# Six mix products in front of the retention, and two tiles' router input made by GpSimd

## The reference, cut to what matters

```python
mod = (silu(c) @ w_ada + b_ada)          # six vectors of 1024: sh1, sc1, g1, sh2, sc2, g2
proj = (x * (1 + sc1) + sh1) @ w_in
y_ssd, y_rg, y_ret = ssd(proj), rglru(proj), retention(proj)     # 1024, 512, 512 features
mix = concat([y_ssd, y_rg, y_ret]) @ w_out                       # 2048 x 1024
x = layernorm(ALPHA * x + (1 + g1) * mix)
h2 = x * (1 + sc2) + sh2
x = layernorm(ALPHA * x + (1 + g2) * moe(h2))                    # router, then 32 experts, top 2 of one group
```

## Time and profile before

| | |
|---|---|
| median of three runs | 1937.51 us |
| the profiled execution: its time, its span | 1933.65 us, 1931.8 us |
| TensorE busy | 1540.0 us (80%) |
| VectorE busy | 752.8 us (39%) |
| ScalarE busy | 348.1 us (18%) |
| GpSimd busy | 113.7 us (6%) |
| chain that ended last | PE 47%, DMA 39%, DVE 6% |

### The profile page before, as it was taken

How to read it: one execution, slowest core, us unless ns; L and a number is a source line. 1 busy time by engine, 2 the same in 40 slices (tenths; PEclk the granted TensorE clock), 3 DMA queues, 4 the chain that set the end, 5 groups by cost and what they waited for, 6 DMA issues and landing times.

```text
span 1931.8 us, 29459 instructions
## 1 busy us (share of the span) xinstructions
PE 1540.0 (80%) x11754; PEld 830.8 (43%) x11754; DVE 752.8 (39%) x1685; ACT 348.1 (18%) x773; POOL 113.7 (6%) x162
## 2 busy tenths in 40 slices
PE   5999999888767677668699999998887767667782
PEld 2764544434433334334266554353453334333441
DVE  0343657567212222122525356666732222122235
ACT  1235311121101111100123532110311111011010
POOL 3000012101000000000020000211000000000000
PEclk8999998988988888888899899998888888788896
DMA  9445346517899999999935433654669999999991
GB/s 328 143 175 179 121 122 205 219 71 290 364 427 427 428 429 428 429 428 427 384 111 198 155 121 121 207 170 163 283 268 427 428 429 429 428 428 428 428 427 78
DMA packets 93463, 567.53 MB, mean 294 GB/s; under 512 B 7061, under 2 KB 7917, under 8 KB 68034
## 3 DMA queue, kind: packets, MB, share of 16 engines
q1 hardware_dynamic: 81666, 532.05, 67.6%
q0 software_dynamic: 11712, 34.32, 6.3%
HBM read 550.53 MB, written 15.81 MB: 293 GB/s over the span
## 4 chain that ended last, share of the span: by engine, by line
PE 47%; DMA 39%; DVE 6%; ACT 2%; issue 2%; SPq 2%; DVEq 2%; PEldq 0%; PEld 0%; ACTq 0%
DMA ring<-in_exp_w_up 37%; PE ps L1445 10%; PE ps L962 9%; PE ps L937 9%; PE ps L1183 3%; PE ps L944 2%; PE ps L1308 2%; DMA ring<-in_w_out 2%; PE ps L863 1%; PE ps L805 1%; PE ps L1420 1%; PE ps L1153 1%; DMA ring<-in_w_ada 1%; PE ps L1088 1%; PE ps L1129 1%
## 5 line engine op out<-in xcount | busy, mean ns | idle before, releaser
L1445 PE MATMUL ps<-ring,xTb 128*32 128x256 f32 x4224 | 326.9, 478 | 240.8 <-DMA ring<-in_exp_w_up 235.6
L1445 PEld LDWEIGHTS ps<-ring,xTb 128*32 128x32 f32 x4224 | 163.0, 136 | 404.1 <-issue 359.8
L2522 DVE TENSOR_TENSOR hb<-sg,ps 128x128 f32<-128x128 f32 x66 | 25.0, 379 | 492.6 <-ACT sg L1784 492.6
L962 PE MATMUL ps<-ring,hT 128*128 128x512 f32 x384 | 171.4, 598 | 0.0
L937 PE MATMUL ps<-hT,ring 128*128 128x288 f32 x640 | 165.4, 418 | 5.9 <-ACT hT L1565 2.4
L1420 PE MATMUL ps<-sel,h_tm 128*128 128x128 f32 (+1 forms) x912 | 163.5, 306 | 0.0
L1420 PEld LDWEIGHTS ps<-sel,h_tm 128*128 128x128 f32 x912 | 125.2, 189 | 53.9 <-issue 26.2
L937 PEld LDWEIGHTS ps<-hT,ring 128*128 128x128 f32 x640 | 122.7, 195 | 44.1 <-issue 9.7
L1459 PE MATMUL ps<-ring,hTb 128*32 128x256 f32 x2112 | 131.0, 389 | 5.1 <-DVEq L2525 5.1
L1784 ACT ACTIVATE sg<-ps 128x128 f32<-128x128 f32 x66 | 18.3, 278 | 596.2 <-PE ps L1445 596.2
L2530 DVE COPY ys<-ps 32x256 f32<-32x256 f32 x132 | 56.0, 424 | 166.0 <-PE ps L1459 164.8
(11 more groups left out here) (444 smaller groups left out, 1617.8 us busy)
## 6 DMA issues: line engine op xcount, KB each, us to landing
ring<-in_exp_w_gate SPq DMA_DIRECT2D x66, 2048.0 KB, 18.8
ring<-in_exp_w_up SPq DMA_DIRECT2D x66, 2048.0 KB, 23.3
ring<-in_exp_w_down SPq DMA_DIRECT2D x66, 2048.0 KB, 24.8
ring<-in_w_ada SPq DMA_DIRECT2D x24, 2048.0 KB, 11.4
ring<-in_w_in SPq DMA_DIRECT2D x22, 2048.0 KB, 9.1
ring<-in_w_out SPq DMA_DIRECT2D x8, 2048.0 KB, 14.7
h0s<-in_state_ssd POOLq DMA_DIRECT2D x16, 512.0 KB, 7.1
out_ssd_s<-h0s POOLq DMA_DIRECT2D x16, 512.0 KB, 5.5
```

The lines of the kernel that those rows point to most:

```text
L962: last = mm(o[:, :], hT[:, k, T0[i]:T0[i] + P], w[:, k, :], start=(k == 0), stop=(k == KT - 1))
L1445: last = mm(ps[32 * j:32 * j + 32, b, 0:2 * P], xTb[:, k, m * BLK:(m + 1) * BLK], w[:, 0:2, k * D_EXPERT + j * P:k * D_EXPERT + (j + 1) * ...
```

## The change: what it does

Two things, in both layers.

1. TensorE does all six products mix_a(0..2, 0..1) before it turns q and k, and releases slots 1 and 2 right behind them. The places in the retention that they leave are filled by ada blocks: block 8 behind the scores of tile 0, block 9 before the turning of tile 0's result, block 10 behind ri of tile 1, and only block 11 in the part of the sample states. The bank list and ScalarE's list follow the same order.
2. h2 of tiles 0 and 2 is made by GpSimd: it waits for sh2 and sc2, then for each of the two tiles a product, a drain and a sum. VectorE signals the tiles that it has normalised and goes on with the last half of tile 1. TensorE waits for GpSimd's signal before it turns tiles 0 and 2, and VectorE waits for it before it writes `rt`, which lies over sc2.

```diff
--- before.py
+++ after.py
@@ ret_steps @@
     if i == 0:
-        out += [(("mix_a", 1, 1), "A"), (("rs", i), "D"), (("mix_a", 2, 0), "A"), (("ri", i), "D"), (("mix_a", 2, 1), "A")]
+        out += [(("ada", 8), "A"), (("rs", i), "D"), (("ri", i), "D")]
     elif i == 1:
-        out += [(("ro", i), "D"), (("rs", i), "D"), (("ada", 8), "A"), (("yrt", 0), "A"), (("ri", i), "D"), (("ada", 9), "A")]
+        out += [(("ro", i), "D"), (("rs", i), "D"), (("ada", 9), "A"), (("yrt", 0), "A"), (("ri", i), "D"), (("ada", 10), "A")]
     else:
-        out += [(("rt", b), "D") for b in range(4)] + [(("yrt", 1), "A"), (("ada", 10), "A"), (("ada", 11), "A")]
+        out += [(("rt", b), "D") for b in range(4)] + [(("yrt", 1), "A"), (("ada", 11), "A")]
@@ bank_plan @@
-    out += [(("yt", 2, a), "A") for a in range(2)] + [(("mix_a", 1, 0), "A")]
+    out += [(("yt", 2, a), "A") for a in range(2)]
+    out += [(("mix_a", i, a), "A") for i in (1, 2) for a in range(2)]
@@ signals @@
-        h2_ready = sig("h2_ready", NT + 1)
+        h2_ready = sig("h2_ready", 2)
+        h2_few = sig("h2_two_tiles_ready", 2)
+        x_normed = sig("two_tiles_normed", 2)
@@ GpSimd, behind the loads of ln1_g and ln1_b @@
+                pool.wait_ge(*takes(l, ("ms", 6)))
+                idle["pool"].stand(pool)
+                for n_, i in enumerate(NORM_ORDER[:2]):
+                    R_, w_ = ROWS[i], int(i == 2)
+                    pool.wait_ge(x_normed.sem, x_normed.at(l, n_ + 1))
+                    pool.tensor_tensor(h_tm[0:R_, i, :].rearrange("r (k p) -> r k p", k=KT),
+                                       x_tm[0:R_, i, :].rearrange("r (p k) -> r k p", k=KT),
+                                       sc2[0:R_, w_, :].rearrange("r (k p) -> r k p", k=KT), ALU.mult)
+                    pool.drain()
+                    pool.tensor_tensor(h_tm[0:R_, i, :], h_tm[0:R_, i, :], sh2[0:R_, w_, :], ALU.add
+                                       ).then_inc(h2_few.sem, 1)
                 pool.wait_ge(x1_done.sem, x1_done.at(l, 1))
@@ TensorE @@
                 turn_rows(h_tm, "yt", 2)
-                mix_a(1, 0)
+                for i in (1, 2):
+                    for a in range(2):
+                        mix_a(i, a)
+                free_slot(n_out)
+                free_slot(n_out + 1)
...
                     if i == 0:
-                        mix_a(1, 1)
+                        pe.wait_ge(bias_in.sem, bias_in.at(l, 32))
+                        ada_here(8)
...
                             if q:
-                                ada_here(10)
                                 ada_here(11)
...
-                    if i == 0:
-                        mix_a(2, 0)
                     if i == 1:
-                        pe.wait_ge(bias_in.sem, bias_in.at(l, 32))
-                        ada_here(8)
+                        ada_here(9)
                         turn_ret(0)
...
-                    if i == 0:
-                        mix_a(2, 1)
-                        free_slot(n_out)
-                        free_slot(n_out + 1)
                     if i == 1:
-                        ada_here(9)
+                        ada_here(10)
...
                 for n_, i in enumerate(NORM_ORDER[:2]):
-                    pe.wait_ge(h2_ready.sem, h2_ready.at(l, n_ + 1))
+                    pe.wait_ge(h2_few.sem, h2_few.at(l, n_ + 1))
                     turn_rows(h_tm, "h2t", i)
@@ VectorE @@
                         norm((i,), 2 * NT + 1 + NORM_ORDER.index(i), ln1_in)
-                        if i == 2:
-                            dve.wait_ge(*takes(l, ("ms", 6)))
-                            modulate(0)
-                            modulate(2)
+                        dve.sem_inc(x_normed.sem, 1)
                 D().then_inc(x1_done.sem, 1)
+                dve.wait_ge(*takes(l, ("ms", 6)))
...
                 pref = over(C("pref"), NT, 1)
+                dve.wait_ge(h2_few.sem, h2_few.at(l, 2))
                 V.memset(rt[:, 0], 0.5)
```

More of the change, by code:

```diff
@@ L1372, in _ @@
                 for a in range(2):
-                    pe.wait_ge(h2_ready.sem, h2_ready.at(l, NT + a))
+                    pe.wait_ge(h2_ready.sem, h2_ready.at(l, a + 1))
                     turn_half(1, a)
@@ L1708, in _ @@
                 take_rows(hT, "yt", 2)
-                take_mix_a(1, 0)
+                for i in (1, 2):
+                    for a in range(2):
+                        take_mix_a(i, a)
                 for i in range(NT):
@@ L1717, in take_ret @@
                     cp(yreT[:, :, T0[i]:T0[i] + R_], o[:, 0:4 * R_].rearrange("p (k t) -> p k t", k=4)).then_inc(TA, 1)
-                take_mix_a(1, 1)
-                take_mix_a(2, 0)
+                take_ada((8,))
                 rstd(NT + 1, ROWS[0], 0, RET_HEADS)
-                take_mix_a(2, 1)
                 act.wait_ge(ada_folded.sem, ada_folded.at(l, 1))
                 cp(adaf, ps[:, 7, :]).then_inc(adaf_ready.sem, 1)
-                take_ada((8,))
+                take_ada((9,))
                 take_ret(0)
                 rstd(NT + 2, ROWS[1], 0, RET_HEADS)
-                take_ada((9,))
+                take_ada((10,))
                 take_ret(1)
-                take_ada((10, 11))
+                take_ada((11,))
                 rstd(NT + 3, ROWS[2], 0, RET_HEADS)
@@ L2275, in _ @@
                 mods(range(4, 6))
-                def modulate(i):
-                    R_, w_ = ROWS[i], int(i == 2)
-                    tt(h_tm[0:R_, i, :].rearrange("r (k p) -> r k p", k=KT),
-                       x_tm[0:R_, i, :].rearrange("r (p k) -> r k p", k=KT),
-                       sc2[0:R_, w_, :].rearrange("r (k p) -> r k p", k=KT), ALU.mult)
-                    D()
-                    tt(h_tm[0:R_, i, :], h_tm[0:R_, i, :], sh2[0:R_, w_, :], ALU.add).then_inc(h2_ready.sem, 1)
                 if l == 0:
```

## The result

The changed kernel takes 1952.61 us (median of 4 runs, 1949.62 to 1954.86) against 1937.10 (1934.17 to 1939.25): a ratio of 1.0090 with a 95% interval of 1.0073 to 1.0106. The medians differ by 15.5 us, and the ratio stands for 14 to 21. The forecast was 1940.1, within 1930.5 to 1947.5. It is outside that range.

What follows compares the result with a forecast made beforehand. The prediction took the path from the retention to the first expert as the bound, experts alternating between TensorE and weight landings. Part 1 at 0 and part 2 at 2 x 1.3 gave 1937.51 + 2.6 = 1940.1 us, range 1930.5 to 1947.5.

Steps and rivals of the forecast that it cites:

- Part 1, 0 us: Retention to mix(0): reordering the six products turns the wait for weights into an equal wait for a bank; 0 us.
- VectorE's serial list: Retention and sample states: VectorE's work runs later, fourth state by 6.1 us, fifth by 5.2 in layer 0, 4.9 in layer 1.
- The wait for the seventh state's bank: Start of mix(0): its first half waits for this bank, taken at 392.7, so TensorE starts at 392.8.
- The price of the two products, kept at 16.42: At mix(0): the two products keep their slow start and still take 16.42 us.
- Rivals C and D: At mix(0): C, full clock, -2.4 per layer, 1935.3, chance 0.15; D, VectorE's list not late, 1926.0, chance 0.06.
- rival B: At h2: GpSimd is as fast as VectorE; -2.3 per layer, 1932.9, chance 0.14.
- Part 2, "the middle, 11.0": At h2 of tiles 0 and 2: GpSimd's four instructions take 11.0 us, fillers before the logits start +1.3 per layer.
- rival A: At h2: GpSimd and VectorE take turns at the same memory, tile 2 2.5 later; +3.8 per layer, 1945.1, chance 0.27.
- The high end (14.7, +5.0 per layer): At h2: GpSimd handles one operand after another with longer hand-overs, 14.7 us; +5.0 per layer, 1947.5.
- Whatever comes before the first expert moves the end one for one: Expert part of each layer: a delay ahead of the first expert shifts the end by the same amount.
- The sum: Whole kernel: 0 plus 2 x 1.3 = +2.6 us on the median 1937.51, giving 1940.1.

Runs made afterwards that it cites:

- part1_only: Kernel before with only the six mix products moved in front, h2 left with VectorE; ratio 1.0007.
- p1_fill2: Kernel before with the six products in front and filler products in TensorE's waits for h2 and around the rank matmuls, second measurement; ratio 0.9976.
- part2_only: Kernel before with only h2 of tiles 0 and 2 given to GpSimd, mix products where they were; ratio 1.0043.
- gp_tile2: Kernel before with six products in front, GpSimd making only tile 2's h2, an early small GpSimd product, and fillers around the rank matmuls; ratio 0.9966.
- after_again: The changed kernel measured once more, for a second profile; ratio 1.0093.
- warm: Changed kernel plus an 8-column product and drain on GpSimd ahead of its wait for the first tile, behind that for sc2; ratio 1.0084.
- fill_gp: Changed kernel with filler products in TensorE's long waits for GpSimd; ratio 1.0070.
- gp_alone: Changed kernel with VectorE waiting for GpSimd's second tile before tile 1's last half; ratio 1.0109.
- fill_rank: Changed kernel with eight fillers for seven ahead of the rank matmuls and three more behind them, before the diagonal's rows; ratio 1.0021.
- p1_trim: Kernel before with six products in front and fillers in TensorE's waits, but one filler for three ahead of the logits, one for two behind; ratio 0.9964.
- warm_rank: Changed kernel with fillers around the rank matmuls and the 8-column GpSimd product straight behind its loads, before all its waits; ratio 1.0008.

## Why the prediction was wrong

- **Part 1, 0 us: right over the whole, in layer 0 with luck.** The wait for w_out went, and VectorE's serial list was late by nearly what was worked out (fifth sample state at 386.26, 387.4 in the clock of before, forecast 387.95). But the first two mix products ran 1.6 us faster here (15.43 for 16.99 us), which no term held. In layer 1, where they took the same (16.66 and 16.78), the fifth state was 6.1 late where 4.9 was forecast, and the product started 1.5 later. The wait for the seventh state's bank was not what ended last. part1_only and p1_fill2 show no cost over the whole.
- **The price of the two products, kept at 16.42: right in layer 0** (16.53; in layer 1 15.46). Rivals C and D fell; rival B fell with GpSimd's pace.
- **Part 2, "the middle, 11.0": mis-sized, and rival A true.** Measured 13.75. Its parts: 10.5 of GpSimd's own work with hand-overs, 2.04 pause, 1.2 of turns. The forecast's middle, 11.0, is near the 10.5, but by luck: it was the middle of two ends of 7.3 and 14.7, with no row near either. The trace of before showed no such pause, and rival A was put at 2.5 where the turns cost 1.2 on the path. The high end (14.7, +5.0 per layer) held it: counted from the start of L837, the fillers came 4.6 and 4.5 later. By this term alone the time is that of part2_only, +0.43%, inside the range.
- **The rule of the Trainium skill** (SBUF — State Buffer, "Who interferes with whom"), that a VectorE instruction with two SBUF inputs and a GpSimd one that reads SBUF exclude each other for a whole instruction, agrees with the traces here: 2.22 for 0.69 us, and 3.66 for 1.21 in gp_tile2, ending 0.5 to 1.1 behind GpSimd's end. It also says that a scalar instruction in the mode of two ports does so; the 2.37 for 0.81 us of L2275 agrees.
- **"Whatever comes before the first expert moves the end one for one": the step that failed.** The sum took a delay in front of the router as a shift of all that follows and put the stretch behind it at nothing. It did not keep its length. Its gather went from 9.15 to 14.90 in one of two layers, in four of the five profiles in which both parts were in and the short waits were not filled (changed kernel, after_again, warm, fill_gp, but not gp_alone), and in none of the other thirteen. I had weighed the granted clock at mix(0) only, and not at the gather, where the windows of before show it at 0.50 up to 1404. fill_rank shows it by taking 14 us away without touching GpSimd's part. Without the 7.5 us of the gather the mis-sized middle alone would have stayed in the range.
- **Open:** why the clock comes back after 8 us of work in one execution and after 25 in another. The waits in front are the same (1.60 and 2.42 us after, 1.58 and 2.43 before). Neither part alone did it to the gather in its profile. A long stay at half doesn't need GpSimd's part, though: p1_trim, which is without it, has one of 16 us in front of the router.

## What to carry to other kernels

Where TensorE's clock falls in front of a stretch of matmuls, that stretch is not a constant: before moving anything ahead of it, read the granted clock there, and price the stretch at half clock as the bad case (here 7.5 us, where the edit costs 4 in a layer). Filling the short wait ahead of it with idle products is worth trying by itself. Work given to GpSimd on the critical path needs its own pace (here 1.4 to 1.9 times VectorE's) and a first instruction made early; work of VectorE that reads two operands from SBUF beside it stood still here (up to 3.66 us for 1.21).

## What the hardware showed that I had not expected

- GpSimd's first arithmetic instruction after its transfers is followed by a pause of 2.04 us, the same in both layers and in every kernel in which nothing goes ahead of it, and gone with the 8-column product 30 us earlier (0.14 us left).
- GpSimd's product of 1024 columns with a strided operand takes 2.85 us, its sum 2.34 alone; 32 rows cost as much as 128 (gp_alone). The sum took 2.60 in warm_rank.
- TensorE, working without a gap of a microsecond from 1405.5 on, stayed at half clock until 1431, where in the kernel before full clock came back 7.8 us after it had begun again.
